# Prompt attention: bias addition and row maximum of a score tile, one vector operation for both heads

## The reference, cut to what matters

```python
lw = jnp.einsum('ntghd,nkgd->ntghk', qg, kw) + bw     # scores + bias, 16 heads of 64
pw = masked_softmax(lw, mw)                           # exp(x - max) / sum
ow = jnp.einsum('ntghk,nkgd->ntghd', pw, vw)
o = gt[..., 0:1] * oc + gt[..., 1:2] * osel + gt[..., 2:3] * ow
```

## Time and profile before

| | |
|---|---|
| time, median of 3 runs | 2373.68 us (2372.03 to 2374.86) |
| span of the profiled execution | 2380.7 us |
| TensorE busy | 95% of the span |
| VectorE, ScalarE, GpSimd busy | 47%, 24%, 46% |
| prompt attention stage | about 222 to 411 us of the span |

### The profile page before, as it was taken

The page is one execution under the profiler, slowest core; times in us unless marked ns, Lnnn a source line. Parts: engine busy times, 40 slices in busy tenths (PEclk is TensorE's granted clock), DMA queues, the critical chain, the costliest instruction groups (busy, mean ns, idle before and its releaser), DMA issues. The chain is left out here.

```text
span 2380.7 us, 37761 instructions
## 1 busy us (share of the span) xinstructions
PE 2273.5 (95%) x14824; PEld 1696.0 (71%) x14824; DVE 1108.5 (47%) x2044; ACT 580.4 (24%) x1340; POOL 1101.9 (46%) x980
## 2 busy tenths in 40 slices
PE   9898999899999999999999999999999999999997
PEld 7675444467777777767777768676776767777776
DVE  5343786535430341367886556453643154302322
ACT  2003666401000000145554324332420010000011
POOL 3211545256564465365654242332425466634653
PEclk9999999989999999999999999999999999999998
DMA  9734000821211211311221020200203112112211
GB/s 325 215 99 153 1 1 3 306 101 58 84 58 71 106 71 71 121 65 61 73 74 56 7 107 6 76 33 23 90 12 140 71 71 71 71 71 90 88 71 40
DMA packets 55883, 197.16 MB, mean 83 GB/s; under 512 B 15458, under 2 KB 29538, under 8 KB 39714
## 3 DMA queue, kind: packets, MB, share of 16 engines
q1 hardware_dynamic: 49186, 177.52, 21.2%
q0 software_dynamic: 3088, 14.03, 1.7%
q10 hardware_dynamic: 3440, 3.25, 0.4%
HBM read 170.86 MB, written 32.17 MB: 85 GB/s over the span
## 5 line engine op out<-in xcount | busy, mean ns | idle before, releaser
L1959 PE MATMUL ps<-xn,ring 128*128 128x288 f32 x768 | 199.0, 407 | 5.4 <-DVE xn L2062 3.2
L1959 PE MATMUL ps<-hid,ring 128*128 128x288 f32 x768 | 192.8, 406 | 0.0
L1959 PEld LDWEIGHTS ps<-xn,ring 128*128 128x128 f32 x768 | 145.3, 190 | 48.3 <-DVE xn L2062 6.0
L1959 PEld LDWEIGHTS ps<-hid,ring 128*128 128x128 f32 x768 | 145.6, 190 | 40.7 <-ACT p L1996 0.8
L2042 POOL TENSOR_TENSOR prod<-prod,rstd 128x1152 f32<-128x1152 f32 x32 | 83.9, 2622 | 179.6 <-DVE prod L2126 163.3
L1996 ACT ACTIVATE p<-ps 128x288 f32<-128x288 f32 x48 | 19.7, 410 | 597.4 <-PE ps L1959 597.4
L3371 PE MATMUL ps<-xn,ring 128*128 128x288 f32 x512 | 137.1, 414 | 3.6 <-PE ps L3440 3.6
L1020 POOL TENSOR_SCALAR ring<-ring,fac 128x128 f32<-128x128 f32 (+2 forms) x96 | 92.5, 980 | 96.1 <-DVE fac L1256 96.1
L1959 PE MATMUL ps<-x_sum,wsum 128*128 128x288 f32 x512 | 131.0, 408 | 2.1 <-DVE x_sum L2066 1.0
L1959 PE MATMUL ps<-hid_sum,wsum 128*128 128x288 f32 x512 | 128.4, 407 | 0.2
L2016 POOL TENSOR_TENSOR wsum<-ring 128x512 f32<-128x512 f32 x64 | 81.9, 1279 | 100.0 <-DMA ring<-in_w_mlp 92.1
(11 more groups left out here) (528 smaller groups left out, 4991.0 us busy)
## 6 DMA issues: line engine op xcount, KB each, us to landing
ring<-in_w_mlp SPq DMA_DIRECT2D x64, 1024.0 KB, 4.8
ring<-in_w_gdn_in SPq DMA_DIRECT2D x16, 1024.0 KB, 4.8
ring<-in_w_nsa_in SPq DMA_DIRECT2D x9, 1024.0 KB, 16.9
ring<-in_w_gdn_z SPq DMA_DIRECT2D x8, 1024.0 KB, 4.9
x<-in_seq_state SPq DMA_DIRECT2D x4, 2048.0 KB, 8.9
out_seq_state<-x SPq DMA_DIRECT2D x4, 2048.0 KB, 11.0
ring<-in_w_gdn_out SPq DMA_DIRECT2D x8, 1024.0 KB, 5.7
out_win_old<-in_win_rows POOLq DMA_DIRECT2D x1, 8064.0 KB, 46.4
```

Of the source, the lines that this page charges most:

```text
L1959: mm = nc.tensor.matmul(S.ps[:, base + BANK[p], 0:HT], stationary(p, blk.units[pair // 4], pair % 4), moving(blk.kind, p, pair), start=pai ...
```

## The change

The two bias additions of a tile become one VectorE instruction over both banks, and the two maxima become one that writes two numbers. The addition waits for the scores of both halves, the maximum for the joint addition. `biased` and `maxed` now count once for a tile, not twice, and both halves of `exp` wait for the same joint maximum.

```diff
             def exp(job, i):
                 k = slot[job, i]
                 for half in range(2):
-                    act.wait_ge(maxed, unit(job, i, half))
+                    act.wait_ge(maxed, job * PT + i + 1)
...
                 n = width(i)
                 w = min(n, 256)
-                for half in range(2):
-                    dve.wait_ge(score, 2 * k + half + 1)
-                    tail = S.ps[:, score_bank(k, half), n - w:n]
-                    v.tensor_tensor(tail, tail, S.toep[:, h0 + 4 * half, 256 - w:256], ALU.add).then_inc(biased, 1)
-                for half in range(2):
-                    dve.wait_ge(biased, unit(job, i, half))
-                    if unit(job, i, half) > 4:
-                        dve.wait_ge(exped, unit(job, i, half) - 4)
-                    v.tensor_reduce(nmax[:, 2 * (i % 2) + half:2 * (i % 2) + half + 1],
-                                    S.ps[:, score_bank(k, half), 0:n], AX, ALU.max, negate=True).then_inc(maxed, 1)
+                both = S.ps[:, score_bank(k, 0):score_bank(k, 0) + 2, :]
+                dve.wait_ge(score, 2 * k + 2)
+                v.tensor_tensor(both[:, :, n - w:n], both[:, :, n - w:n], S.toep[:, h0:h0 + 5:4, 256 - w:256], ALU.add
+                                ).then_inc(biased, 1)
+                dve.wait_ge(biased, job * PT + i + 1)
+                if job * PT + i >= 2:
+                    dve.wait_ge(exped, unit(job, i, 1) - 4)
+                v.tensor_reduce(nmax[:, 2 * (i % 2):2 * (i % 2) + 2], both[:, :, 0:n], AX, ALU.max, negate=True
+                                ).then_inc(maxed, 1)
```

## The result

| | median | runs | ratio to before, 95% interval |
|---|---|---|---|
| before | 2374.27 us | 4 (2372.03 to 2375.71) | |
| changed | 2392.26 us | 4 (2387.7 to 2394.8) | 1.0071 [1.0056, 1.0085] |
| changed, timed again | 2390.93 us | 6 (2388.71 to 2394.38) | 1.0074 [1.0059, 1.0089] |

The change makes the kernel slower by 0.7%, 17 us by the means of all timed runs, where 9.2 were forecast. The first measurement, 2392.26 us, lies above the forecast range, which ended at 2391; the median of the repeat, 2390.93 us, lies at its upper end.

What follows compares the result with a forecast made beforehand. The prediction took a closed loop VectorE, ScalarE, TensorE, set by start-to-result delays, to bound the stage. Delays of 5.4 + 2.8 + 1.0 = 9.2 us on a median of 2373.7 gave 2383 us, range 2377.5 to 2391.

Steps and rivals of the forecast that it cites:

- The prices of joint instructions: VectorE in the stage: joint maxima of 1024, 512, 256 columns 1214, 681, 410 ns; joint additions 691 and 423 ns.
- (a): s3 of the even job, through reciprocal and scalings to s1 of the odd job: +0.60 us, nine times, 5.4 us.
- (b): s1 of the odd job, through copies, transposes and `qk` to the bias of s3: +0.35 us, eight times, 2.8 us.
- (c): s0 of the even job, through copies, transposes and `qk` to the bias of s2: +0.19 us, five rounds, 1.0 us.
- (d): s3 of the odd job: its +0.60 us is covered by 3.6 us before its factors are needed, cost 0.
- Sum: 5.4 + 2.8 + 1.0: Total of the delays on the stage's loop, from s3 even, s1 odd and s0 even: 9.2 us.
- For five it is 5 x 0.19: s0 of the even job counted in five rounds, leaving out three with a low-clock stretch about there: 1.0 us.
- Rival 1: Longer rounds bring two to six more low-clock stretches on TensorE, 1.3 us each: 2385.5 to 2391 us; chance 0.19.
- Rival 2: The stage's loop has slack hidden by one round, so only part counts: +2 to +5.4 us, 2376 to 2379; chance 0.16.
- Rival 3: VectorE's throughput limits and the joint maximum follows its addition without waiting: 9 us faster, 2365 us; chance 0.06.
- Rival 4: Crossing banks costs 0.148 us per joint instruction, 0.9 us a round, 7 us more: 2390 us; chance 0.04.

## Why the prediction was wrong

**Right.** The direction, and the reading behind it: the stage is a closed loop through VectorE, ScalarE and TensorE, VectorE gains nothing from fewer instructions, and the first exponential is what is lost. The prices of joint instructions, the crossing of banks taken at nothing, (a), (b), (c) and (d) came within 0.05 us. That the additions and maxima cost when joined on three tiles (23.60 us) and next to nothing on four others (22.07 us) is shown; so is that the loss comes with the maximum.

**Wrong: the size, 9.2 us for 17.** The step that failed is the sum itself: it put at nothing every instruction that the change does not touch, and it left out the clock. Three terms.

1. "Sum: 5.4 + 2.8 + 1.0". It holds only instructions that the change touches. A shift of all that follows in the queue by 0.2 us (c) put an untouched one, the mask's multiplication, on the start of a GpSimd scaling: 0.36 us in a clean round, 2.2 us over six such rounds. That is an upper end. In the changed kernel's rounds with a stretch at the low clock the multiplication stays at 0.41 us: of seven rounds six have it slow in the first profile and three in the repeat. No row that I had chosen could have shown the collision, but GpSimd's scalings could have been asked for, and I never laid a moved instruction against them.
2. "For five it is 5 x 0.19". The step (c) was there in every clean round, 0.2 us long: three times 0.2 us more. With that and the first term the forecast would be 12.0 us. The lengths of the stage add up to the same: first bias to first reciprocal, first round, six clean rounds, last reciprocal are 8.5 + 21.55 + 6 x 22.03 + 9.0 = 171.3 us before and 9.7 + 21.87 + 6 x 23.61 + 10.0 = 183.2 after, 11.9 more. The stage as it ran in the two profiles, low stretches included, grew by 11.9 us too (175.1 to 187.0). That the totals agree is in part luck: the first length grew by 1.1 us where 0.60 was priced, and the first round by 0.32 where the full 1.14 and more was.
3. Rival 1, the clock, had a size that holds the measured one (2 to 6 stretches more, at 1.3 us, are 2.6 to 7.8 us; 3.4 of the 17 go with the lower mean clock) and was treated wrongly: as an alternative to the forecast. It is an addition to it. That this size fits is luck in part, since its reason, more such stretches in the longer rounds, is not what the profiles show. Added up, the range would have reached past the result. The 1.7 us between the stage's 11.9 and the 13.6 at equal clock I can't place.

Rival 2 (slack) is refuted by the tile s3 alone, +0.60 of 0.60, and by (b) and (c), which came in full. Rival 3 (faster) by VectorE's busy time of 18.38 us a round against 18.24. Rival 4 (crossing at 0.148 us) by 11 to 14 ns.

The rule of the Trainium skill ("VectorE: DVE Perf Modes", "Rules for kernel authors") to keep the number of operations small gave, with that page's fixed cost, 16 us of VectorE as an estimate; the page of the profile shows 1.1 us for 128 instructions. The prediction says that the trace disagrees with the Trainium skill on independent pairs. That was read too narrowly: the same paragraph of "The DRAIN you can't avoid" adds that a next operation which is not held starts earlier, and the pairs of the kernel before, overlapping by 0.09 us, agree with it.

## What to carry to other kernels

Joining two instructions can pay where the engine's sum of work is the limit. Where a loop through several engines is the limit, as here, it trades the first result for the last, and the first is what the next engine waits for. Price it from start to first result, per tile, and check which tiles the loop passes: here three of eight carried the whole of it, and a fourth was hidden behind them. And a forecast for a loop needs two more things: every instruction that the shift moves against another engine's instructions, and the clock as a term of the sum, not as another story.

## What the runs showed of the hardware

- A VectorE multiplication of two SBUF operands, 248 columns, takes 406 ns in the kernel before, where GpSimd is busy beside it too, and 770 ns when it starts 0.07 us behind the start of a GpSimd scaling of 384 columns (1.24 us, unchanged). So it is the moment that counts, not that GpSimd is busy. Two more cases are less clear. With GpSimd's order changed, a VectorE instruction on eight columns grew from 0.17 to 0.33 us in three of eight jobs. In the changed kernel with late scalings, VectorE's two scalings of 512 columns take 1.42 or 1.20 us together, where they take 1.01 in the kernels with early ones, beside GpSimd in both. Neither was tested.
- A VectorE maximum over two PSUM banks costs 11 to 14 ns more than the line through single banks, and an addition over two banks takes 692 ns where a two-operand instruction of the same size that reads one bank takes 691.
- With no edit at all the program's time follows its mean granted clock, 1.46 us for each 0.001 (0.983 to 0.991 in 56 runs of the kernel before, the two levels being 1.2 and 2.4 GHz).
- A stretch at the low level costs 1.3 us in a round of 22.03 us. In the repeated profile of the changed kernel it seems to cost less, rounds of 24.28 to 24.34 us against 23.60; but in these rounds the mask's multiplication takes 0.41 us, as the collision with GpSimd does not happen. Against the 23.24 us of a round without the collision (23.60 - 0.36, an estimate) the stretch costs some 1.05 to 1.1 us.
